# A two-layer hybrid encoder in split float32: large on-chip buffers moved to other addresses modulo 128

## What is computed

```python
for i in range(DEPTH):
    hn = rmsnorm(h, attn_norm[i])
    qkv = hn @ w_qkv[i]                                   # 1024 x 2304
    ya = sliding_window_sink_attention(...)               # 8 heads, 2 key/value heads
    yb = chunked_relpos_attention(...)                    # 8 heads, 9 chunks of 64
    h = h + jnp.concatenate([ya, yb], axis=-1) @ w_o[i]
    h = h + conv_gated_mlp(rmsnorm(h, ffn_norm[i]), w_up[i], conv_w[i], conv_b[i], w_down[i])
    gate = jax.nn.sigmoid(rmsnorm(h, ple_norm[i]) @ w_ple_gate[i])
    h = h + (p[i] @ w_ple_proj[i]) * gate
```

## Time and profile before

| what | value |
| --- | --- |
| median of 3 runs | 2586.57 us (2586.46 to 2590.55) |
| profiled execution, span from first to last instruction | 2581.1 us |
| that execution's own time | not listed apart; the median of the runs stands 5.5 us over its span |
| TensorE busy (x matmuls) | 2543.9 us (x13328) |
| weight loads busy | 2188.4 us |
| VectorE / ScalarE / GpSimd busy | 1380.2 / 1308.9 / 1016.2 us |
| granted TensorE clock, mean | 1.000 |

### The profile page before, as it was taken

One profiled execution on the slowest core, in us unless ns is written; L12 is line 12 of the kernel. 1 busy time (PEld: TensorE's weight loads), 2 busy tenths in 40 slices (PEclk: granted clock), 3 DMA queues, 4 the chain that ended last, 5 costly groups with the idle time before them and its releaser, 6 DMA issues.

```text
span 2581.1 us, 41875 instructions
## 1 busy us (share of the span) xinstructions
PE 2543.9 (99%) x13328; PEld 2188.4 (85%) x13328; DVE 1380.2 (53%) x2073; ACT 1308.9 (51%) x2190; POOL 1016.2 (39%) x749
## 2 busy tenths in 40 slices
PE   8999999999999999999999999999999999999999
PEld 7999998777888888888899999987778888888887
DVE  3114675176556567873241156742766566777732
ACT  4335775275555554334353367743755555533342
POOL 3444221238787760001124443201487787400011
PEclk9999999999999999999999999999999999999999
DMA  4111000223233248431111110003133333573312
GB/s 157 46 49 42 27 2 18 90 66 122 78 110 117 78 156 297 131 106 42 37 44 44 47 36 28 10 18 114 50 106 105 94 106 105 173 276 115 98 49 82
DMA packets 179770, 223.85 MB, mean 87 GB/s; under 512 B 7952, under 2 KB 110736, under 8 KB 179632
## 3 DMA queue, kind: packets, MB, share of 16 engines
q1 hardware_dynamic: 179040, 219.66, 26.8%
q0 software_dynamic: 592, 2.46, 0.3%
HBM read 169.08 MB, written 55.36 MB: 87 GB/s over the span
## 4 chain that ended last, share of the span: by engine, by line
PE 93%; DVE 2%; issue 2%; ACT 1%; POOL 1%; DMA 0%; ACTq 0%; DVEq 0%; SPq 0%; POOLq 0%
PE ps L2045 10%; PE ps L2046 10%; PE ps L2047 10%; PE ps L2409 10%; PE ps L2412 10%; PE ps L2411 10%; PE ps L2433 6%; PE ps L2435 6%; PE ps L2254 6%; PE ps L2434 6%; PE ps L2205 3%; PE ps L2235 3%; PE ps L2180 2%; PE ps L2084 1%; DMA h<-in_x 0%
## 5 line engine op out<-in xcount | busy, mean ns | idle before, releaser
L823 POOL TENSOR_TENSOR w_hl<-w_raw,w_hl 128x1024 fp32r<-128x1024 f32 x84 | 201.6, 2400 | 1025.6 <-ACT w_hl L998 1025.6
L2045 PE MATMUL ps<-w_hl,xT 128*128 128x384 f32 (+1 forms) x1280 | 463.0, 362 | 1.3 <-DVE xT L1524 1.1
L2047 PE MATMUL ps<-w_hl,xT 128*128 128x384 f32 (+1 forms) x1280 | 459.8, 359 | 0.0
L2046 PE MATMUL ps<-w_hl,xT 128*128 128x384 f32 (+1 forms) x1280 | 459.7, 359 | 0.0
L998 ACT ACTIVATE w_hl<-w_raw 128x1024 fp32r<-128x1024 f32 x84 | 89.1, 1061 | 431.6 <-PE ps L2047 403.9
L2045 PEld LDWEIGHTS ps<-w_hl,xT 128*128 128x128 f32 x1280 | 240.1, 188 | 25.8 <-DVE xT L1524 3.2
L2047 PEld LDWEIGHTS ps<-w_hl,xT 128*128 128x128 f32 x1280 | 240.1, 188 | 23.5
L2046 PEld LDWEIGHTS ps<-w_hl,xT 128*128 128x128 f32 x1280 | 240.2, 188 | 22.0
L1541 DVE TENSOR_REDUCE q_sum<-sq 128x384 f32 x80 | 44.2, 553 | 271.9 <-ACT sq L1054 271.9
L1853 DVE SCALAR_TENSOR_TENSOR ps<-c_up,ccols,ps 128x1023 f32<-128x1023 f32 x84 | 107.8, 1283 | 152.4 <-ACT ps L1308 152.4
L1114 ACT ACTIVATE probs<-scores,neg_max 128x192 f32<-128x192 f32 (+5 forms) x256 | 144.3, 565 | 36.2 <-DVE neg_max L1613 35.5
(11 more groups left out here) (271 smaller groups left out, 6272.9 us busy)
## 6 DMA issues: line engine op xcount, KB each, us to landing
ad_raw<-v_rows SPq DMA_DIRECT2D x70, 512.0 KB, 3.7
raw_a<-in_w_up SPq DMA_DIRECT2D x44, 512.0 KB, 5.0
raw_g<-in_w_up SPq DMA_DIRECT2D x44, 512.0 KB, 5.2
v_rows<-c_up SPq DMA_DIRECT2D x22, 1024.0 KB, 4.4
w_raw<-in_w_qkv SPq DMA_DIRECT2D x48, 384.0 KB, 3.2
wd_main<-in_w_down SPq DMA_DIRECT2D x30, 512.0 KB, 7.7
v_rows<-hc_g SPq DMA_DIRECT2D x22, 512.0 KB, 5.0
w_raw<-in_w_o SPq DMA_DIRECT2D x16, 512.0 KB, 3.3
```

The costliest lines, as they stand in the source:

```text
L823: nc.gpsimd.tensor_tensor(w_hl[:, slot % 2, 1, :], w_raw[:, slot % 2, :], w_hl[:, slot % 2, 0, :].bitcast(F), ALU.subtract) \
L2045: nc.tensor.matmul(dst, lhs[:, k, 0, cols], wh, start=first, stop=False)
L2046: nc.tensor.matmul(dst, lhs[:, k, 0, cols], wl, start=False, stop=False)
L2047: return nc.tensor.matmul(dst, lhs[:, k, 1, cols], wh, start=False, stop=last)
```

## The change

The buffers w_hl, bd_two, bd_two_raw and ring_four, which lie over each other, are allocated with 8 elements more (32 bytes), and used from their fifth element on, so their data start 16 bytes later. Everything behind them moves up by 32 bytes. A new buffer half_line of 16 elements (64 bytes), which nothing uses, lies ahead of the last region. In all the last region moves up by 96 bytes.

```diff
-        w_hl = sb("w_hl", [P, 2, 2, 1024], R, r0)
+        w_hl = sb("w_hl", [P, 4 * 1024 + 8], R, r0)[:, 4:4 + 4096].rearrange("p (a b n) -> p a b n", a=2, b=2)
...
-        bd_two = sb("bd_two", [P, 2, 2, 2, HALF], R, r0)
+        bd_two = sb("bd_two", [P, 8 * HALF + 8], R, r0)[:, 4:4 + 4096].rearrange("p (a b c n) -> p a b c n", a=2, b=2, c=2)
...
-        bd_two_raw = sb("bd_two_raw", [P, 2, 2, 2, HALF], F, r0)
+        bd_two_raw = sb("bd_two_raw", [P, 8 * HALF + 8], F, r0)[:, 4:4 + 4096].rearrange("p (a b c n) -> p a b c n", a=2, b=2, c=2)
...
-        ring_four = sb("ring_four", [P, 4, 2, HALF], R)
+        ring_four = sb("ring_four", [P, 8 * HALF + 8], R)[:, 4:4 + 4096].rearrange("p (a b n) -> p a b n", a=4, b=2)
...
         v_nat = sb("v_nat", [P, 2, TT, HD])
+        sb("half_line", [P, 16])
```

## The result

| | before | after |
| --- | --- | --- |
| median | 2586.53 us (12 runs, 2583.12 to 2590.55) | 2592.94 us (12 runs, 2592.71 to 2593.85) |
| ratio | | 1.0023, 95% interval 1.0015 to 1.0032 |
| span of the profiled execution | 2581.1 us | 2590.9 us |

The changed kernel is 0.23% slower, 6.4 us between the medians.

The account below looks back on a forecast made before the run. TensorE was taken as the bound, time being matmul count times step. Savings of 38.1 us took the span from 2581.1 to 2543.0 us, plus 5.5 us for the median: 2548.5 us, with an 8-in-10 range of 2480 to 2602 us.

Parts of the forecast that it names:

- I take 227.0 ns for 16 and 48 apart: Products whose operands become 16 or 48 bytes apart: 512-column step falls to the equal pairs' 227.0 ns; likeliest case, chance 0.36.
- the sum of 38.1 us: Savings over all products: 9.9 us at 384 columns, 11.4 w_hl at 512, 7.4 bd_two, 6.4 x_four, 3.0 x_two.
- The scaling to 384 columns: w_hl with xT, 384 columns: hold-up scaled by 0.68, step from 173.3 to 169.0 ns, 9.9 us saved over 2304 matmuls.
- For 64 apart I keep 229.2: x_four with ring_three, equal before and 64 apart after: step stays 229.2 ns, between 227 and 233.3, costing nothing.
- rival D: Slower: only equal residues are cheap, every other distance costs 233.3 ns, losing 7.4 us in the gated MLP; 2594.0 us, chance 0.25.
- The steps of 229.2 and 230.0 in equal pairs: Gated MLP before the change: x_four with ring_three at 229.2 ns and x_two with ring_four at 230.0, taken as their prices.
- if its first products no longer stand above 227: Condition on x_two with ring_four, 16 apart after the change, saving 3.0 us over 1008 matmuls.
- if the equal pairs change too, for then it was not the pairing: Sign that the forecast is wrong: pairs equal before and after, bd_one with ad and x_one with ring_three, change their steps.
- hold-ups of 20.2 and 13.7 ns: Time over the 213.3 ns streaming time of 512 columns, read as weight-load delay: 20.2 in differing pairs, 13.7 in equal ones.
- dearer end of 49 us: Extra loss in rival D if 16 apart is dearer than 32 by another 6.6 ns (4.3 at 384 columns); 2643 us.
- Rival B: Cheaper still: equal pairs' hold-up also shrinks; half gone gives 2504.6 us, all gone (213.3 ns) 2460 us; chance 0.24.
- Rival C: No effect: the residue that counts is coarser or something else, gains and losses cancel; 2586.6 us, chance 0.15.

Follow-up runs that it names:

- all_equal: Kernel before with only 32 bytes of padding ahead of ident, putting every large buffer at 0 modulo 128; 2553.35 us, ratio to before 0.9875.
- minus_sixteen: Changed kernel with 16 elements of padding in place of 8 and without half_line; 2597.75 us, ratio to before 1.005.
- map_fine: Matmuls alone, one loaded and one moving buffer, the moving slice read every 4 bytes through 256; 226.7 to 240.0 ns a step at 512 columns.
- last_thirtytwo: all_equal with 32 bytes of padding ahead of the last region only; 2571.85 us, ratio to before 0.995.
- no_half: Changed kernel without half_line, low data at 16, middle and last region at 0; 2572.55 us, ratio to before 0.9948.
- no_sixteen: Changed kernel without the 16-byte shift: all_equal plus half_line, last region at 64 modulo 128; 2573.1 us, ratio to before 0.9952.
- map_order: Matmuls alone, 512 columns, each pair run behind two different pairs in turn; the same 24 matmuls took 5.68 us in one section, 5.45 us in another.

## Why the prediction was wrong

**What bounds the kernel: right.** TensorE's steps are the time, and the waits and the other engines stayed where they were. That the relation between the two operands sets the step was right as well: every run of the study moves the time by addresses alone, over 44 us from all_equal to minus_sixteen.

**The step that failed** is "I take 227.0 ns for 16 and 48 apart", with its reason that small distances are nearer to the cheap row at 0. The price is not a slope. bd_two, 48 apart, stands at 234.8 ns; w_hl, 16 above xT, at 231.7; the pairs 16 below ring_four at 226.7 to 234.2, by what runs before them. Direction was missing as well: map_fine has 231.7 ns for 16 above and 236.7 for 16 below, 233.4 for 48 above and 235.0 for 48 below, and the change brought only w_hl to the cheaper side. Term by term, against the sum of 38.1 us: x_four with ring_four -6.4 forecast, +0.4 measured; bd_two -7.4, +1.5; w_hl at 512 columns -11.4, -2.5; x_two -3.0, +0.8. (The trace has 1080, 1056 and 1032 matmuls of x_four with ring_four, x_two with ring_four and x_four with ring_three, where the sum took 1008 of each; that is under 1 us.)

**The scaling to 384 columns** failed in sign: -9.9 us forecast, +5.1 measured. I assumed that 384 columns at 32 apart pay the same hold-up as 512 do. They pay no more than an equal pair does: all_equal brings 6.6 ns a step at 512 columns and nothing at 384 (400.0 us against 399.9), and 32 apart was one of the best distances there is for 384 columns. The earlier trace rows could not tell this; a long run of 384 columns on an equal pair didn't exist before.

**"For 64 apart I keep 229.2"**, costed at 0, cost 4.2 us directly. I had bounded it by 233.3 and priced that end at 4.1 us in rival D, so only the choice was wrong (map_fine has 228.9 for 64 above, but 233.3 for 64 below, and the change made it 64 below). What neither I nor a rival had is its effect on others: with everything else held, the half_line costs 20.2 us, half of it in pairs that it doesn't touch.

**The steps of 229.2 and 230.0 in equal pairs** The earlier trace rows were read as the price of these pairs, "if its first products no longer stand above 227" hinting at more. They were equal pairs recovering from a dear neighbour: all_equal has the same pairs at 226.7. So one sign of being wrong, "if the equal pairs change too, for then it was not the pairing", was itself too narrow. x_one with ring_three did change, from 123.1 to 124.0 us, and all_equal with 122.7 and last_thirtytwo with 123.9 us speak for the pairs ahead of it as the cause. No run shows the 213.3 and 160.0 ns from which the hold-ups of 20.2 and 13.7 ns are counted.

**Rival D** named 2594.0 us and 2592.94 was measured, by luck and by other terms than its own: it had x_two +3.3 and x_four with ring_three +4.1 and all else unchanged; measured against the trace were +0.8 and +4.2, with +5.1 at 384 columns that it had not. Its statement, only equal residues are cheap, comes nearest of the four for a pair alone at 512 columns, once "equal" is read modulo 256, though eleven other distances of map_fine stand at 228.7 to 230.0 ns and not at 233.3; for pairs in a sequence no_half breaks it. Its dearer end of 49 us speaks of 16 apart alone, but the sum takes in the pairs 48 and 64 apart too. Rival B's end of 213.3 ns was never approached: nothing in 64 distances is below 226.7. Rival C, no effect of the pairing, is refuted by all_equal, though gains and losses did nearly cancel here.

The Trainium skill, "TensorE: Matmul & The Clock Gate", says in Part 2, step one, that weights and moving operand come through two independent ports, so that loading weights takes nothing from the running matmul. By that every layout here would take the same time. The runs disagree: 226.7 to 240.0 ns in map_fine, where only the address of the moving operand changes, and 1.7% between the two ends of the full kernels. Under Back-to-back issue gap the same page of the Trainium skill gives some 216 ns for 512 columns, as the gap of an isolated matmul at the full clock, and some 131 ns for each matmul in a stream with weight loads. No run here settled under 226.7 ns at 512 columns.

## What stays open

- Why the unit is 256 bytes, why equal addresses settle at 226.7 ns, and what the state is that is carried from pair to pair. The runs show that it exists and what it costs, not where in the chip it sits. That the weight load holds up the running matmul is the prediction's reading. The relation of the two addresses fits it, but no run left the weight loads out.
- Moving one pair alone. The low buffers w_hl, bd_two and ring_four overlie each other and take over each other's space slot by slot, so shifting one against the others would have needed other synchronization. It wasn't tried.
- The runs of before fall into three levels, about 2583, 2586.5 and 2590 us, while every other layout keeps within 1.9 us (apart from two executions of no_sixteen, at granted clocks of 0.58 and 0.95) and all_equal within 0.7. Several steady rhythms for one layout would do that; it is only argued.

## What to carry to other kernels

Place the two operands of long series of fp32r matmuls at equal addresses modulo 256 bytes; here 32 bytes of padding in front of ident did it, and took 1.25% off (2553.35 us), all of it in matmuls of 512 columns. A table that is added or resized shifts everything behind it, so look at the addresses after such an edit, and don't guess at a distance from its neighbours: measure the step, start to start over dozens of matmuls, in the sequence in which the pairs really run. If TensorE bounds a kernel and its steps lie a few per cent over the best pair's, that is the place to look.

## What was unexpected of the hardware

- The step of an fp32r matmul of 512 columns, with a weight load for each, depends on the moving address less the loaded address modulo 256, to 4 bytes. In the one sequence of map_fine it settles at 226.7 ns at 0, 238.8 at 4, 231.7 at 16, 240.0 at 68, 233.3 at 128.
- The same unequal pair has several steady steps. The one 16 below its partner ran at 226.7, 233.3 or 236.7 ns, by what came before, and kept to the dear one over 95 steps in a row (map_order).
- 384 columns spread less, 173.3 to 180.0 ns, and nine of the 32 distances tried have the least step. They are not the best ones of 512 columns: 32 apart costs nothing at 384 and 6.6 ns at 512.
